# Delta rule on one Trainium2 core: the gate products of the next pass on VectorE, in levels four and five, in place of GpSimd

## The reference

```python
def step(s, xs):
    qc, kc, vc, gc, bc = xs
    gcum = jnp.cumsum(gc, axis=-1)
    decay = jnp.exp(jnp.where(tri, gcum[..., :, None] - gcum[..., None, :], -jnp.inf))
    kk = jnp.einsum('bhid,bhjd->bhij', kc, kc)
    m = jnp.where(strict, bc[..., :, None] * kk * decay, 0.0)
    rhs = jnp.concatenate([vc * bc[..., None], kc * (bc * jnp.exp(gcum))[..., None]], axis=-1)
    sol = lax.linalg.triangular_solve(eye + m, rhs, left_side=True, lower=True, unit_diagonal=True)
    ...
```

## Time and profile before

| | before |
|---|---|
| median of three runs | 3315.28 us (3314.7 to 3319.97) |
| the profiled execution, its own time | 3318.51 us |
| span of that execution | 3316.7 us |
| PE busy | 2888.5 us, 87% |
| DVE busy | 1700.7 us, 51% |
| ACT busy | 1152.5 us, 35% |
| POOL busy | 355.8 us, 11%, all of it from the delta stage on apart from a few set-up instructions |

### The profile page before, as it was taken

One profiled execution on the slowest core, in us unless ns is written; L12 is line 12 of the kernel. 1 busy time (PEld: TensorE's weight loads), 2 busy tenths in 40 slices (PEclk: granted clock), 3 DMA queues, 4 the chain that ended last, 5 costly groups with the idle time before them and its releaser, 6 DMA issues.

```text
span 3316.7 us, 44150 instructions
## 1 busy us (share of the span) xinstructions
PE 2888.5 (87%) x16684; PEld 2334.3 (70%) x16684; DVE 1700.7 (51%) x2844; ACT 1152.5 (35%) x2037; POOL 355.8 (11%) x567
## 2 busy tenths in 40 slices
PE   5968689999686699699988999986899996999699
PEld 2725468887364699378867888875688883886699
DVE  1345554333235656288336777775434441449665
ACT  2314242222323444243244544543322231432443
POOL 0000000000000000000006666640000000005000
PEclk8988799999798799899979999997999997999799
DMA  9310022223730245832310000012222228220254
GB/s 384 115 38 1 13 78 100 89 99 110 294 117 1 91 178 187 320 114 96 127 58 1 1 1 2 1 46 82 76 93 98 89 101 338 84 83 1 102 179 150
DMA packets 49885, 343.08 MB, mean 103 GB/s; under 512 B 5328, under 2 KB 7376, under 8 KB 9808
## 3 DMA queue, kind: packets, MB, share of 16 engines
q1 hardware_dynamic: 44528, 317.74, 26.3%
q10 hardware_dynamic: 5216, 23.44, 1.8%
HBM read 333.82 MB, written 7.34 MB: 103 GB/s over the span
## 4 chain that ended last, share of the span: by engine, by line
PE 76%; DVE 10%; DMA 6%; ACT 4%; issue 3%; DVEq 0%; POOL 0%; ACTq 0%; SPq 0%; POOLq 0%
PE ps L492 18%; PE ps L493 17%; PE ps L494 17%; DMA ring<-in_w_dram 6%; PE ps L1732 3%; PE ps L1719 3%; PE ps L541 2%; PE ps L1711 2%; PE ps L1740 1%; PE ps L520 1%; ACT H L466 1%; PE ps L1674 1%; PE ps L599 1%; DVE ring_rest L480 1%; PE ps L1761 1%
## 5 line engine op out<-in xcount | busy, mean ns | idle before, releaser
L494 PE MATMUL ps<-hidden_high,ring_rest 128*128 128x256 f32 (+2 forms) x1384 | 464.4, 336 | 0.0
L492 PE MATMUL ps<-hidden_high,w_high 128*128 128x256 f32 (+1 forms) x1160 | 388.4, 335 | 11.7 <-DVE h_rest L488 8.8
L492 PE MATMUL ps<-h_high,w_high 128*128 128x512 f32 (+1 forms) x1024 | 350.7, 342 | 29.8 <-DVE h_low L1262 26.3
L1270 DVE TENSOR_TENSOR ring_rest<-ring,w_high 128x2048 fp32r<-128x2048 f32 x124 | 284.3, 2292 | 161.4 <-ACT w_high L930 161.4
L493 PE MATMUL ps<-h_low,w_high 128*128 128x512 f32 (+1 forms) x1024 | 350.1, 342 | 0.0
L494 PE MATMUL ps<-h_high,ring_rest 128*128 128x512 f32 (+1 forms) x1024 | 348.1, 340 | 0.0
L493 PE MATMUL ps<-hidden_low,w_high 128*128 128x512 f32 (+1 forms) x1024 | 346.5, 338 | 0.0
L930 ACT ACTIVATE w_high<-ring 128x2048 fp32r<-128x2048 f32 x124 | 236.7, 1909 | 302.1 <-PE ps L494 302.1
L494 PEld LDWEIGHTS ps<-hidden_high,ring_rest 128*128 128x128 f32 (+1 forms) x1384 | 263.0, 190 | 30.5 <-issue 0.6
L2010 POOL TENSOR_SCALAR RS<-C,arena 128x128 f32<-128x128 f32 x128 | 74.9, 604 | 1747.4 <-DVEq L1634 1747.4
L492 PEld LDWEIGHTS ps<-hidden_high,w_high 128*128 128x128 f32 x1160 | 218.2, 188 | 40.4 <-issue 9.7
(11 more groups left out here) (384 smaller groups left out, 5891.3 us busy)
## 6 DMA issues: line engine op xcount, KB each, us to landing
ring<-in_w_dram SPq DMA_DIRECT2D x302, 1024.0 KB, 4.9
z_spill<-arena ACTq DMA_DIRECT2D x16, 256.0 KB, 2.1
arena<-z_spill ACTq DMA_DIRECT2D x4, 1024.0 KB, 8.6
C<-in_first_dram ACTq DMA_DIRECT2D x1, 2432.0 KB, 21.0
X<-in_x_dram ACTq DMA_DIRECT2D x1, 2048.0 KB, 13.2
x_spill<-X ACTq DMA_DIRECT2D x1, 2048.0 KB, 8.2
X<-x_spill ACTq DMA_DIRECT2D x1, 2048.0 KB, 15.6
C<-in_third_dram ACTq DMA_DIRECT2D x1, 2048.0 KB, 15.6
```

Of the source, the lines that this page charges most:

```text
L492: ins = nc.tensor.matmul(out_, w_high, high, start=first, stop=False)
L494: return ins, nc.tensor.matmul(out_, w_rest, high, start=False, stop=last)
L1270: nc.vector.tensor_tensor(RING_REST[:, v.place(j + 1)], ring[:, v.place(j + 1)], W_HIGH[:, (j + 1) % 2, :].bitcast(F32), ALU.subtract).the ...
```

## The change

The four instructions of each `gate` are issued by DVE instead of POOL. Before the loop DVE makes the gates of both units of the first pass. In the loop, DVE makes those of unit 0 for the next pass in level four and those of unit 1 in level five, each between the two masks and the two additions of that level. POOL made them at the end of levels two and four. The wait for `am` and the semaphore `gate` stay as they were.

```diff
--- before.py
+++ after.py
@@ dve_delta
+            def gate(i, u):
+                d, c, hp = PASSES[i]
+                if i:
+                    dve.wait_ge(sems[f"am{u}"], i)
+                for h in range(4):
+                    ins = nc.vector.tensor_scalar(RS[:, u, h * P:(h + 1) * P], cst("incl", d * P, d * P + P), col(SG_, d, c, hp, u, h), None, ALU.mult)
+                ins.then_inc(sems[f"gate{u}"], 1)
...
             for u in range(2):
+                gate(0, u)
+            for u in range(2):
                 first(0, u)
...
                     for u in range(2):
                         mask_y(i, n, u)
+                    if n in (4, 5) and i < LAST:
+                        gate(i + 1, n - 4)
                     for u in range(2):
                         move(i, n, u)
@@ pool_delta
-            def gate(i, u):
-
-                d, c, hp = PASSES[i]
-                if i:
-                    pool.wait_ge(sems[f"am{u}"], i)
-                for h in range(4):
-                    ins = nc.gpsimd.tensor_scalar(RS[:, u, h * P:(h + 1) * P], cst("incl", d * P, d * P + P), col(SG_, d, c, hp, u, h), None, ALU.mult)
-                ins.then_inc(sems[f"gate{u}"], 1)
...
             for u in range(2):
-                gate(0, u)
                 keys(0, u)
...
                     if 2 < n < 5 and i < LAST:
                         keys(i + 1, n - 3)
-                    if n in (2, 4) and i < LAST:
-                        gate(i + 1, n // 2 - 1)
```

## The result

| | before | changed |
|---|---|---|
| median of five runs each | 3315.28 us (3310.79 to 3319.97) | 3333.03 us (3326.55 to 3337.7) |
| ratio to before | | 1.005, 95% interval 1.0032 to 1.0068 |
| profiled execution, its own time | 3318.51 us | 3327.68 us |
| span of that execution | 3316.7 us | 3325.9 us |
| delta stage | 481.00 us | 495.15 us |

The change makes the kernel slower by 17.75 us in the medians; the forecast was 15.1 us, 3330.4. The delta stage is measured here from the start of DVE's clearing of the state (line 1896) to the end of its last addition to the output (line 1974, 1983 in the changed kernel), and split at the start of `first` for unit 0. Within the profiled executions the stage grew by 14.15 us: -1.89 in its start part and +16.04 in the rest.

What follows compares the result with a forecast made beforehand. In levels four and five, DVE's addition for unit 0 was taken to release PE's next level without slack. The loop's +17.4 us and the start's -2.3 us gave +15.1 us, 3330.4 us on the 3315.28 us median; range 3322 to 3338.

Steps and rivals of the forecast that it cites:

- PE's next level waits for unit 0's addition without slack: Levels four and five: DVE's addition for unit 0 releases PE's next level; lateness passes on fully, 0.58 us each time.
- Price of a gate: Gates on DVE in the loop: 0.21 us each, from 0.14 without a column plus 0.07 for it; four take 0.83 us.
- A: Rival, short pitch in the loop: the column's read overlaps, each gate costs 0.14 us; +7.0 us, 3322; chance 0.11.
- B: Rival, long pitch in the loop: each gate costs 0.25 us, as with a PSUM source; +20.5 us, 3336; chance 0.10.
- DVE's own gap of 0.25 us: Levels four and five, before unit 0's addition: 0.25 us free, gates push it by 0.58 us; 30 times, 17.4 us.
- Gates off POOL gain nothing: Loop: POOL's 30 groups of four gates, 2.34 us each, are covered by PE's levels; removing them gains zero.
- The start: Start of the stage: idle DVE makes the first gates sooner, -2.3 us once; 1.8 if POOL's copies interfere, otherwise 2.5.
- Rival C: DVE and POOL block each other: a copy under way costs DVE's gates up to 0.40 us; +12 us, 3342; chance 0.07.
- The sum: Whole kernel: +17.4 us in the loop and -2.3 us at the start give +15.1 us, 3330.4 us (+0.46%).

Runs made afterwards that it cites:

- one per gap: Against the changed kernel, the loop's gates stand singly behind masks and additions of levels three to five: stage 479.08 us, whole time 3320.59 us, ratio 0.9999 to the kernel before.
- the first experiments: Four kernels, ratios to the kernel before: only the first pass's gates on DVE 0.9984, only the loop's 1.0037, one gate per gap 0.9999, all eight in level four 1.0045.
- the keys beside the gates: Against the changed kernel, POOL's key copies wait for the second mask of levels four and five, to start together with DVE's gates: stage 503.95 us.
- the gates behind the additions: Against the changed kernel, the four gates of levels four and five stand behind the two additions instead of in front: stage 485.96 us.
- the constant: Against the changed kernel, the loop's gates multiply by -1 instead of a column of scalars, first pass unchanged: stage 486.96 us.
- the kernel where POOL waits: Against the changed kernel, POOL waits at the stage's start until both units' first gates are made before copying keys: stage 493.46 us.

## Why the prediction was right

- *PE's next level waits for unit 0's addition without slack.* Right: PE starts 0.06 us behind it before and after, the chain now names DVE there, and the gates cost in front of it and not in the gaps beside it (one per gap). The reading that mattered was the 1.25 against 0.89 us in the earlier trace rows: the busy time by stretch had shown PE at 98%, and still there were 0.36 us per level in which DVE held it. Not all of them lie in front of line 1711: by the starts of the timeline before (PE's products at 2153.65 and 2154.31, line 1711 at 2154.85, with 0.44 us for a product that nothing holds) about 0.22 us are PE's wait for unit 1's mask and at least 0.10 us its wait for unit 0's addition. The forecast needed only that the second is not zero.
- *Price of a gate.* 0.21 us taken, 0.195 measured. It was built from 0.14 without a column and 0.07 for the column; they measured 0.135 and 0.06. A (0.14) and B (0.25) are both out: the column's read is not hidden, and with the source in SBUF the gate is cheaper than the 0.25 us of the earlier trace rows, where it is in PSUM.
- *DVE's own gap of 0.25 us.* Right: 0.78 - 0.54. The term was 30 x 0.58 = 17.4 us and measured 16.0 us, all of the difference from the gate's price.
- *Gates off POOL gain nothing.* Right, to 0.05 us.
- *The start.* -2.3 us taken, -1.9 measured, within the 1.8 to 2.5 given. The matmuls of line 1674 followed each other as worked out; DVE's gates came late because of POOL's copies (0.64 us), which was the reason given for the smaller figure. That the figure is so near is in part luck: this term also holds the moment at which PE's clock rises, which the prediction did not reckon with. PE began unit 0's products of keys 2.12 us earlier in the stage, but they took 1.91 us instead of 1.68. With the same start two other kernels had a start part of 8.56 and 8.57 us, a gain of 3.0 us.
- *Rival C.* Its condition, a copy under way as the gates start, was not met in the loop: POOL's key copies ended 1.76 us after the start of level four, as worked out (2153.95 - 2152.20 = 1.75). It was met at the start. Its price, up to 0.40 us for one copy, was too high: a copy beside the gates cost 0.15 us.
- *The sum.* +15.1 us forecast, +14.15 us in the stage: the loop's term was 1.4 us too large, the start's gain 0.4 us too large. The medians differ by 17.75 us, with an interval from 10.6 to 22.5 us that holds both. The whole time can't confirm the forecast more closely than that: the kernel before alone had medians of 3315.28 us here and 3320.18 us beside the first experiments. The profiles show no further change outside the stage that could belong to the gates: that part was 4.9 us shorter in the changed kernel's profiled execution, well inside its own wandering.

## What to carry to other kernels

Work that is moved to an engine with much idle time costs nothing only if each piece fits into the gap that is there at its place in that engine's order. Read the gap in front of the instruction that releases the bound engine, subtract it from what is put there, and charge the rest in full each time; the same instructions, one per gap over three levels, were free here and cost 16 us four at a time. An engine that reads as 98% busy may still be held by another in every round: compare the same group of instructions at a place where nothing can hold it.

## What the runs showed of the hardware that was not expected

**Beside POOL's copies the gates are held up, and not for the copies' whole time.** Beside a POOL copy a gate's distance to the next grew from 0.195 to about 0.35 us (2.94 us for eight against 1.66), while the copies kept their time (0.74 or 0.75 us for two in all the rows above, 0.40 us for one). In the earlier trace rows it was the other engine that was held up: POOL's copy took 1.31 us beside DVE's predicated copy. The Trainium skill ("SBUF — State Buffer", the section on two separate sides) says that one of the two has the shared ports for its whole instruction and the other fully blocks. That one of the two is held up agrees with these runs, the extent doesn't: taking strict turns at their usual distances, a gate and a copy would need 0.195 + 0.34 us per pair (0.34 is the step between two of POOL's keep copies in the trace of the keys beside the gates, from 2127.35 to 2127.69), and they needed about 0.36 us. Part of a gate evidently goes on beside the copy. The ends of the instructions say more. The second gate of the group above and POOL's first copy (timeline, trace of the keys beside the gates):

```profile
2125.93 0.40 POOL L2022 COPY X<-arena 128x256 f32<-128x256 f32 x1 [1.00 <-DVE H L1935]
...
2125.98 0.43 DVE L1905 TENSOR_SCALAR RS<-C,arena 128x128 f32<-128x128 f32 x1
```

The gate takes 0.43 us instead of 0.28 and ends 0.08 us behind the copy. So it is each time: in the traces of the change, of the gates behind the additions, of the constant and of the keys beside the gates, 122 gates took 0.42 us or more, and every one of them ended 0.08 to 0.09 us after the end of a POOL copy. A gate that can't finish before the copy does, but whose first part runs beside it, would give just this. But the first gate of the group (2125.78, 0.28 us) was under way when the copy started, and neither took longer than usual. No run changed the length of either, so this reading stays an inference.

**The moment at which PE's clock rises moved the start by 1.1 us.** In the changed kernel PE's granted clock was 0.50 (the lower of its two levels, 1.2 GHz) from 1752.4 to 1757.7, through unit 0's products of keys, and 0.88 on average from there to 1759.0; in the kernel where POOL waits it was 0.50 up to 1753.0 and already 0.91 in the next two microseconds. Before, PE had stood idle for 5.57 and 4.93 us and then begun the products of line 1674, in either. The four products of unit 0's keys took 1.91 us in the first and 1.03 in the second. Kernels whose start was the same word for word (the change, and the constant in place of the column) had start parts of 9.63 and 8.56 us with these two durations. Of the seven kernels with this start, five had 9.54 to 9.64 us and two, the constant and the gates behind the additions, 8.56 and 8.57. So a difference of a microsecond at the start of this stage proves nothing, unless the granted clock there is read first.
